# Constant matrix products on TensorE between the stages of a two-block transformer kernel

## What is computed

```python
# first block, per layer
h = rmsnorm(x, ffn1_pre_g[l])
x = x + 0.5 * rmsnorm(swiglu(h, w_gate, w_up, w_down), ffn1_post_g[l])
h = rmsnorm(x, mix_pre_g[l])
x = x + rmsnorm(hybrid_mixer(h, ...), mix_post_g[l])
h = rmsnorm(x, ffn2_pre_g[l])
x = x + 0.5 * rmsnorm(swiglu(h, ...), ffn2_post_g[l])
# second block, per layer and stage: shift, scale and gate come from a condition vector
y = swiglu(modulate(x, sh1, sc1), ...)
x = layer_norm(ALPHA * x + 0.5 * (1 + g1) * y, ln_gain, ln_bias)
```

## Time and profile before

| what | us |
|---|---|
| median of 3 runs | 2339.51 |
| lowest and highest | 2334.57, 2341.19 |
| the profiled execution, its own time | 2342.36 |
| its span from the first to the last instruction | 2340.5 |
| PE busy in the span | 2197.4 |
| mean granted PE clock | 0.956 of full |

### The profile page before, as it was taken

One profiled execution on the slowest core, in us unless ns is written; L12 is line 12 of the kernel. 1 busy time (PEld: TensorE's weight loads), 2 busy tenths in 40 slices (PEclk: granted clock), 3 DMA queues, 4 the chain that ended last, 5 costly groups with the idle time before them and its releaser, 6 DMA issues.

```text
span 2340.5 us, 34380 instructions
## 1 busy us (share of the span) xinstructions
PE 2197.4 (94%) x12860; PEld 1951.2 (83%) x12860; DVE 1660.6 (71%) x2124; ACT 1152.0 (49%) x1459; POOL 42.7 (2%) x44
## 2 busy tenths in 40 slices
PE   8998998799999989988999999898999999998997
PEld 7888897688878888976888888887888888887886
DVE  6776756678778767666777787776878656777567
ACT  5554533455555445334545545545544545545454
POOL 0000000000000000000000000000000000000000
PEclk9998988799999989987999999999999999999999
DMA  8764321187567743201775676433774555433543
GB/s 322 293 253 179 112 87 37 34 316 270 223 262 270 272 148 121 85 24 67 296 291 190 266 283 266 145 130 128 280 302 162 184 210 209 151 126 118 206 177 146
DMA packets 59268, 447.18 MB, mean 191 GB/s; under 512 B 6961, under 2 KB 7345, under 8 KB 8497
## 3 DMA queue, kind: packets, MB, share of 16 engines
q1 hardware_dynamic: 59184, 446.02, 51.3%
HBM read 444.95 MB, written 1.05 MB: 191 GB/s over the span
## 4 chain that ended last, share of the span: by engine, by line
PE 83%; DVE 13%; ACT 3%; issue 1%; DMA 0%; SPq 0%; DVEq 0%
PE ps L242 27%; PE ps L335 15%; PE ps L247 14%; PE ps L341 7%; PE ps L302 2%; PE ps L296 2%; PE ps L297 2%; DVE w_lo L199 2%; DVE tok L636 1%; PE ps L223 1%; PE ps L224 1%; PE ps L229 1%; DVE arena L1334 1%; PE ps L316 1%; PE ps L973 1%
## 5 line engine op out<-in xcount | busy, mean ns | idle before, releaser
L199 DVE TENSOR_TENSOR w_lo<-raw,w_hi 128x1024 fp32r<-128x1024 f32 x670 | 809.9, 1230 | 375.7 <-ACT w_hi L192 375.4
L192 ACT ACTIVATE w_hi<-raw 128x1024 fp32r<-128x1024 f32 x670 | 694.3, 1052 | 490.1 <-PE ps L341 157.3
L242 PE MATMUL ps<-hT,w_hi 128*128 128x512 f32 x2752 | 687.9, 392 | 0.0
L242 PEld LDWEIGHTS ps<-hT,w_hi 128*128 128x128 f32 x2752 | 500.0, 189 | 92.8 <-ACT w_hi L192 0.3
L247 PEld LDWEIGHTS ps<-hT,w_lo 128*128 128x128 f32 x2752 | 375.4, 190 | 26.8
L247 PE MATMUL ps<-hT,w_lo 128*128 128x256 f32 x2752 | 383.7, 282 | 0.0
L335 PE MATMUL ps<-w_hi,act_hi 128*128 128x512 f32 x656 | 203.7, 392 | 0.0
L335 PE MATMUL ps<-w_hi,act_lo 128*128 128x512 f32 x656 | 202.6, 390 | 0.0
L341 PE MATMUL ps<-w_lo,act_hi 128*128 128x512 f32 x656 | 175.3, 389 | 0.0
L1711 DVE SCALAR_TENSOR_TENSOR arena<-arena,cond 128x1024 f32<-128x1024 f32 x144 | 168.6, 1221 | 2.1 <-DMA arena<-in_w_ada 2.1
L296 PE MATMUL ps<-w_hi,hT 128*128 128x256 f32 (+1 forms) x576 | 147.6, 292 | 0.0
(11 more groups left out here) (327 smaller groups left out, 2541.3 us busy)
## 6 DMA issues: line engine op xcount, KB each, us to landing
raw<-in_g SPq DMA_DIRECT2D x88, 1024.0 KB, 4.8
raw<-in_u SPq DMA_DIRECT2D x88, 1024.0 KB, 4.9
raw<-in_d SPq DMA_DIRECT2D x88, 1024.0 KB, 6.8
arena<-in_w_ada SPq DMA_DIRECT2D x48, 1536.0 KB, 7.5
raw<-in_w_in SPq DMA_DIRECT2D x54, 1024.0 KB, 4.9
raw<-in_w_out SPq DMA_DIRECT2D x16, 1024.0 KB, 4.8
rows<-in_rows SPq DMA_DIRECT2D x13, 1024.0 KB, 8.9
arena<-in_con SPq DMA_DIRECT2D x1, 1344.0 KB, 11.0
```

The lines of the kernel that those rows point to most:

```text
L192: nc.scalar.activation(w_hi[:, buf, 0:width], raw[:, slot, half * UNIT:half * UNIT + width], ACT.Copy).then_inc(unit_hi, 1)
L199: nc.vector.tensor_tensor(w_lo[:, buf, 0:width], raw[:, slot, half * UNIT:half * UNIT + width], w_hi[:, buf, 0:width].bitcast(F32), ALU.su ...
L242: nc.tensor.matmul(o, h_[:, k, c], hT[:, :, 4 * half + k, :], start=(half == k == 0), stop=False)
```

## The change

A helper `keep(n)` issues n matrix products of constants (the identity matrix against the upper triangular matrix and its neighbour, both read as bf16: 128x128 by 128x512) into bank 5. Nobody reads the result, and the next stage's first product into bank 5 overwrites it. Calls of it stand in `pre_pe` and `pre2_pe`, and two new waits of PE order them: for "gained1" and for `x_ready` of tile 1 in the first block, for "t0" (the first eight of L636) in the second. Nothing is removed.

```diff
+    def keep(n):
+        for _ in range(n):
+            nc.tensor.matmul(ps[:, 5, :], IDENT.bitcast(BF16)[:, 0:P], TU.bitcast(BF16), start=True, stop=True)
+
     def pre_pe(pe, g):
+        if g:
+            keep(11)
+            pe.wait_ge(post_v.sem, post_v.at("gained1", g - 1))
+            keep(5)
+            pe.wait_ge(x_ready, g * 16 + 16)
+            keep(4)
         for tile in range(TILES):
             pe.wait_ge(pre_rv.sem, pre_rv.at(f"tok{tile}", g))
             for k in range(KT):
...
                     last.then_inc(pre_t.done("trans1a"), 1)
+            if g and tile == 0:
+                keep(3)
         last.then_inc(pre_t.done("trans1b"), 1)
+        if g:
+            keep(2)
...
     def pre2_pe(pe, g):
+        if g > 6:
+            keep(7)
         for name, tile, b in PIECES:
             if b.start == 0:
                 pe.wait_ge(x_ready, g * 16 + 8 * tile + 8)
             for k in range(4 * b.start, 4 * b.stop):
                 last = nc.tensor.transpose(tile_bank(tile)[:, k // 4, k % 4, :], x[:, tile, k * P:(k + 1) * P], IDENT)
             last.then_inc(pre_t.done(f"trans{name}"), 1)
+            if name == "0":
+                keep(6 if g == 6 else 3)
+        keep(6)
+        pe.wait_ge(pre2_v.sem, pre2_v.at("t0", g - 6))
+        keep(5)
```

## The result

The changed kernel takes 2325.27 us (median of 5 runs, 2323.18 to 2329.33) where the kernel before takes 2339.51 (5 runs, 2334.57 to 2341.19). The ratio is 0.9944, with a 95% interval of 0.9929 to 0.9959: 13.1 us less, between 9.6 and 16.6.

A forecast was written before the change was run, and what follows sets the result against it. PE was taken to bound the kernel (83% of the chain), losing clock after idle norms. Clock held gives 9.0 + 8.4 = 17.4 us, less 0.3 makes 17.1: 2339.51 - 17.1 = 2322.4 us, range 2314 to 2333.

The forecast's parts named there:

- The price of a product: On PE at full clock, one added product takes 0.23 us, with bounds of half and twice that.
- all groups lie beside the norm: At the entries, products fit into PE's idle time during the norm; all groups cost nothing with the clock held.
- The 0.3 us taken off for products that end behind their event: At the entries, some products end just behind the event PE waits for; 0.3 us deducted from the 17.4 us gain.
- The clock held: At all eleven entries, transposes and first units run at full clock; 9.0 us less in the first block.
- L260's first start: At first-block entries, it comes about 0.9 us earlier after the stage's end; in the second block at an unchanged distance.
- The second block's sum: At the entries of stages 6 to 11, first matmuls at full clock save 8.4 us in all.
- Passed on to the end: In feed-forward stages and mixers, an earlier entry carries VectorE with it, so the whole entry gain reaches the end.
- the second rival: In the mixers, VectorE's own work sets the length; gains of stages 1, 4, 7, 10 vanish: 2331 us; chance 0.12.
- A stage 1 that is shorter by about 2.7 us: Sign of the forecast: the first block's first mixer, up to its end, is shorter by about 2.7 us.
- The first: At second-block entries, the clock falls again in two idle pieces, losing the 8.4 us: 2330.8 us; chance 0.10.
- The third: At first-block entries, transposes do not keep the clock; 4.65 us of slow units are lost: 2327 us; chance 0.05.
- The fourth: At the entries, constants don't hold the clock and the products delay transposes, 9 us in all: 2348.5 us; chance 0.06.

The follow-up runs named there:

- e1: Changed kernel with products only in the first block, none at the second block's entries; ratio to the kernel before 0.9965 (0.9953 to 0.9976).
- e2: Changed kernel with products only in the second block, none at the first block's entries; ratio to the kernel before 0.9974 (0.9964 to 0.9983).
- e5: Changed kernel with every group of products twice as long, in the same places; 2347.4 us in one execution.
- e3: Changed kernel with the same products in the same places, each of 16 moving columns instead of 512; 2346.3 us in one execution.
- e4: Changed kernel with both operands of every product read from a tile of zeros; 2327.7 us in one execution.
- e6: Changed kernel without the products between the two tiles' transposes in both blocks and without the two behind the first block's transposes; 2324.8 us in one execution.
- e8: Changed kernel with products in one lump (20 at a first-block stage's end, 11 behind the second block's transposes), without the new waits; 2326.8 us in one execution.
- e12: The changed kernel measured again, unaltered, beside three others; median 2326.54 us, ratio to the kernel before 0.9939 (0.9922 to 0.9957).
- e7: Changed kernel without products ahead of the first block's transposes or behind the second block's; only the inner groups stay; 2347.8 us in one execution.
- e10: Changed kernel plus products at the end of the first block's mixers and twelve among their 48 matmuls of 20 columns; 2317.13 us, ratio to before 0.9900.
- e11: e10 plus 24 products where PE waits 6.9 us for VectorE in the middle of the first block's mixers; 2315.92 us, ratio to before 0.9893.

## Why the prediction was right, point by point

**What bounds the kernel.** Right. The chain's shares did not move, and an entry shortened where products held the clock at it (e1, e2).

**The price of a product.** 0.23 us was taken, 0.215 measured (e5's 8.6 us for 40), and that all groups lie beside the norm held: PE waited 0.35 us for `tok`, where 0.4 was forecast. e5 shows the price once the cover is gone. The 0.3 us taken off for products that end behind their event did not show at stage 8, where the second transposes start 5.5 us after the stage's end in both kernels.

**The clock held.** Right at all eleven entries of the profile, and on the first block's sum to 0.1 us (9.0 against 9.08): transposes 0.87 us earlier, then `hT_hi`, `hT_lo`, entry; and 1.9 and 0.5 us of slow units gone. The closeness is partly luck: the forecast was built on the very execution that it is compared with, and in e2 the same five entries without products come to 66.41 us, not 68.35. One sign came out smaller: L260's first start moved by 0.53 us in the feed-forward stages, not 0.9. The other 0.34 went with L260 itself, 2.49 to 2.15 us, in the middle of which the kernel before had waited for "lo1a". The mechanism is shown by e3, where 16 columns in place of 512 leave the entries slow with everything else the same; e4 shows that the data do not matter.

**The second block's sum.** The one term that was mis-sized: 8.4 us forecast, 7.8 measured; stages 7, 8, 10 and 11 each gave 0.1 to 0.2 less. The price of eight first matmuls at full clock was taken as 1.09 us, which is that of eight transposes. Chain in order of time in the changed kernel, entry of stage 8; it answers to the earlier trace rows:

```profile
1606.16 1.22 PE ps L260 x8
```

That is 1.22 us for 1.09, and it enters at stages 7 to 10, once each; the next two groups took 0.96 and 1.84, where 0.95 and 1.84 were put.

**Passed on to the end.** Right in kind: in feed-forward stages to 0.02 us, and e1's first-block gain reached the end. But I treated the mixers' bodies as fixed, and they are not. In the twelve bodies of stages 1 and 4 with the first block's entries held (changed kernel, e1, e4, e6, e8, e12) I find 232.2 to 239.6, mean 236.9; in the eight without (before, e2, e3, e7) 236.7 to 237.8, mean 237.6. In the mean the entries' gain stays, and a scatter of some 7 us per mixer comes on top. In single executions a body can take much of it back: stage 4's is 239.4 to 239.6 in five of the six with held entries, 1.7 us longer than before, with 58 us at 0.50 for 54.6. "A stage 1 that is shorter by about 2.7 us" was 8.4 in the profile, and stage 4 was 1.0. By the table of bodies that goes with the clock, and not with VectorE's own work, which the second rival had named.

**The size as a whole.** 17.1 us were forecast; the entries give 16.9, the medians 14.2 and 14.7, the ratio's interval 9.6 to 16.6. What lies between 16.9 and some 14 us is not settled. The profile before was of an execution 2.85 us above its median, with a stage 1 entry 1.9 us longer than in e2 or e3; the profile after was 2.1 below its own; the bodies scatter; and a fall at stage 6 as in e12 costs 1.45 us in some executions. That 17.1 came so near to 16.9 says little of what a median execution gains.

**The rivals.** The first (a fall in the double wait of the second block) is real but rare: 1.45 us at 1 of 42 entries, and at stage 6 of e8. What the prediction held against it was one-sided: behind the same wait of 1.98 us stage 10's transposes ran at half clock. The second (mixers absorb it) fell with e1. The third, that transposes do not keep the clock, fell with e6: with only transposes between idle 0.60 and 0.34 us the entries stayed at full pace. Stronger still is the rise in the kernel before. At stage 10 PE did nothing but 16 transposes, without a gap, while the clock was at 0.50, and it was at 1.00 behind them (stretches as in the earlier trace rows):

```profile
2006.00:2009.30 3.30, 3.30 (x16) 3.09 (x16) 2.24 (x6) 0.48 (x3) 0.00 (x0) 0.50 0.43 70
2009.50:2012.70 3.20, 0.09 (x1) 0.00 (x0) 3.20 (x11) 1.69 (x2) 0.00 (x0) 1.00 0.61 253
```

That full clock does not engage for transposes is the Trainium skill's statement ("TensorE: Matmul & The Clock Gate", Part 4: PE-mode transpose). The measurement decides against it here, for these float32 transposes of 128x128, which the trace records as MATMUL.

The fourth fell with e4. e7 has the clock lost and products between the transposes: its feed-forward entries came out 1.1, 0.4 and 1.0 us longer than before, where the rival had put 1.1 to 1.4, and the mixers' shorter. That rival also took one distance for all, a fall 4.5 us after a stage's end; it was 4.6 and 4.4 at stages 1 and 4, but 2.3 at stage 3.

## What to carry to other kernels

Where TensorE must idle for some microseconds in a serial part, look at what it does first afterwards and at which granted clock: the idle time itself is covered, the half-speed work behind it is not. Wide products of constants into a free bank, placed in the idle time and no longer than it, buy that back; put them ahead of the first work after a long wait, and make them wide: as many instructions of 16 columns did nothing (e3). Look for the same loss inside stages, behind narrow matmuls too.

## What the runs showed of the hardware that was not expected

A fully busy PE can lose its clock. Timeline of PE in the changed kernel's narrow unit:

```profile
222.04 0.26 PE L296 MATMUL ps<-w_hi,hT 128*128 128x20 f32 x1
222.15 0.26 PE L297 MATMUL ps<-w_hi,hT 128*128 128x20 f32 x1
...
223.44 0.37 PE L297 MATMUL ps<-w_hi,hT 128*128 128x20 f32 x1
223.65 0.37 PE L296 MATMUL ps<-w_hi,hT 128*128 128x20 f32 x1
```

Matmuls of 20 columns follow each other every 0.11 us, with no gap; the clock falls in the middle of them, they come every 0.21 us from there, and it stays at 0.50 over 222.7 to 232.9 (the last row of the stretches of the changed kernel, above). Twelve wide products among them held it (e10).

This is no single case. In the twelve profiles whose narrow unit has no products the clock falls at all 24 places (stages 1 and 4), 2.3 to 5.6 us after the first of the 48 matmuls; in e10 and e11 it falls at none of four. PE is busy without a break in both cases (16.00 of 16.00 us in e10's stretch), so busy time alone does not hold the clock. That it is the 512 columns of the products, and not that they are bf16, is argued and not shown.

The same kernel's mixer bodies come out at 232.2 us in one place and 239.5 in another of the same execution (changed kernel, stages 1 and 4). What differs between them is where the clock was at 0.50: 41 us of the body in the one, 58 in the other. With e10's products in the mixers both bodies were 232.6 and the five runs lay within 2.8 us, where those of the changed kernel (e12, six runs) lay 11.3 apart: with the table of bodies under "Where the time went" that points to the clock as the source of much of this kernel's scatter.

Operands of nothing but zeros keep the clock at 1.00 like any others (e4).
